# A two-layer mixer block and an attention block on one core: GpSimd's power products issued in four parts, and one reduction moved up

## The reference

```python
for layer in range(2):
    xn = rms_norm(h, attn_norm_g[layer])
    u_ssm, u_g, v_g, q, k, v = split(xn @ w_in[layer])
    y_ssm  = s5_mixer(u_ssm, ...)          # complex diagonal state space, 16 groups x 64 states
    y_sgu  = spatial_gating(u_g, v_g, ...)
    y_diff = diff_attention(q, k, v, ...)  # below
    h = h + concat(y_ssm, y_sgu, y_diff) @ w_out[layer]
    h = h + conv_gated_mlp(rms_norm(h, ffn_norm_g[layer]), ...)

def s5_mixer(...):
    a_bar = exp(lam * dt)
    b_bar = ((a_bar - 1) / lam) * b_mat
    states = associative_scan(a_bar, b_bar u)    # x_t = a x_(t-1) + b u_t, complex
    y = real(states @ c_mat) + d_skip * u
    y = gelu(y); return y * sigmoid(y @ w_glu + b_glu)

def diff_attention(...):
    q, k = rope(rms_norm(q)), rope(rms_norm(k))
    w = softmax(q1 k1) - lam * softmax(q2 k2)    # masked by chunks of 64
    out = w @ v
    return rms_norm(out, sub_gain) * (1 - lambda_init)
```

## Time and profile before

| | |
|---|---|
| profiled execution | 983.3 us, span 981.5 us |
| PE busy | 954.1 us, 97% of the span |
| weight loads (PEld) | 838.0 us, 85% |
| VectorE | 690.5 us, 70% |
| ScalarE | 547.4 us, 56% |
| GpSimd | 263.2 us, 27% |
| weight pairs | 294 loads of 512 KB, 3.5 us each to landing |
| chain that ended last | PE 86%, VectorE 8%, ScalarE 2%, GpSimd 1%, issue 1% |

### The profile page before, as it was taken

How to read it: one execution, slowest core, us unless ns; L and a number is a source line. 1 busy time by engine, 2 the same in 40 slices (tenths; PEclk the granted TensorE clock), 3 DMA queues, 4 the chain that set the end, 5 groups by cost and what they waited for, 6 DMA issues and landing times.

```text
span 981.5 us, 15775 instructions
## 1 busy us (share of the span) xinstructions
PE 954.1 (97%) x6139; PEld 838.0 (85%) x6143; DVE 690.5 (70%) x1074; ACT 547.4 (56%) x900; POOL 263.2 (27%) x196
## 2 busy tenths in 40 slices
PE   5979999999999999999999999999999999999997
PEld 4867789999978887899999988899777889888886
DVE  6998658776764689676777764558575845666785
ACT  7736556665744656766655654553444454555723
POOL 4891101677800021200555400003131300000030
PEclk9999999999999999999999999999999999999999
DMA  7722355655655552556655566565545445754462
GB/s 287 230 85 87 108 174 191 186 183 174 190 190 154 173 168 86 177 168 194 184 192 183 185 192 194 184 204 175 167 149 150 142 153 169 196 167 152 147 186 84
DMA packets 48473, 165.95 MB, mean 169 GB/s; under 512 B 6544, under 2 KB 7056, under 8 KB 48400
## 3 DMA queue, kind: packets, MB, share of 16 engines
q1 hardware_dynamic: 48400, 164.95, 53.0%
HBM read 162.83 MB, written 1.05 MB: 167 GB/s over the span
## 4 chain that ended last, share of the span: by engine, by line
PE 86%; DVE 8%; ACT 2%; POOL 1%; issue 1%; DMA 0%; DVEq 0%; POOLq 0%; SPq 0%; ACTq 0%
PE PJ L605 14%; PE PJ L607 13%; PE PJ L606 13%; PE PJ L596 10%; PE PJ L598 10%; PE PJ L597 10%; DVE wlo L1710 2%; PE PJ L557 2%; PE PJ L559 2%; PE PJ L558 2%; PE T L1045 1%; PE T L1036 1%; PE S L652 1%; DVE ropeq L1821 1%; PE T L974 1%
## 5 line engine op out<-in xcount | busy, mean ns | idle before, releaser
L1710 DVE TENSOR_TENSOR wlo<-raw,whi 128x1024 fp32r<-128x1024 f32 x294 | 366.9, 1280 | 87.1 <-ACT whi L1104 84.8
L1104 ACT ACTIVATE whi<-raw 128x1024 fp32r<-128x1024 f32 x294 | 302.5, 1062 | 73.6 <-DMA raw<-weights_in 64.7
L596 PE MATMUL PJ<-xthb,whi 128*128 128x256 f32 x864 | 243.1, 281 | 0.9 <-DVE wlo L1710 0.5
L598 PE MATMUL PJ<-xthb,wlo 128*128 128x256 f32 x864 | 242.3, 280 | 0.0
L597 PE MATMUL PJ<-xtlb,whi 128*128 128x256 f32 x864 | 241.5, 280 | 0.0
L605 PE MATMUL PJ<-whi,xthb 128*128 128x512 f32 (+1 forms) x432 | 174.3, 403 | 3.6 <-DVE wlo L1710 3.6
L607 PE MATMUL PJ<-whi,xtlb 128*128 128x512 f32 (+1 forms) x432 | 167.9, 389 | 0.0
L606 PE MATMUL PJ<-wlo,xthb 128*128 128x512 f32 (+1 forms) x432 | 167.7, 388 | 0.0
L596 PEld LDWEIGHTS PJ<-xthb,whi 128*128 128x128 f32 x864 | 163.0, 189 | 1.7 <-issue 1.5
L597 PEld LDWEIGHTS PJ<-xtlb,whi 128*128 128x128 f32 x864 | 163.0, 189 | 0.2
L598 PEld LDWEIGHTS PJ<-xthb,wlo 128*128 128x128 f32 x864 | 162.9, 189 | 0.0
(11 more groups left out here) (402 smaller groups left out, 1342.1 us busy)
## 6 DMA issues: line engine op xcount, KB each, us to landing
raw<-weights_in SPq DMA_DIRECT2D x294, 512.0 KB, 3.5
rt<-bmerge_in SPq DMA_DIRECT2D x6, 256.0 KB, 4.4
xres<-x_in SPq DMA_DIRECT2D x2, 512.0 KB, 5.5
memx<-mem_in SPq DMA_DIRECT2D x2, 512.0 KB, 4.1
y_out<-xn SPq DMA_DIRECT2D x4, 256.0 KB, 2.3
rowv<-rows_in SPq DMA_DIRECT2D x1, 576.0 KB, 10.5
ptmp<-bexp_in SPq DMA_DIRECT2D x2, 256.0 KB, 6.3
cex<-cexp_in SPq DMA_DIRECT2D x2, 256.0 KB, 8.5
```

The lines of the kernel that those rows point to most:

```text
L596: pe.matmul(o, a, xh[:, k, :], start=(first and f % 2 == 0), stop=False, skip_group_check=True)
L598: m = pe.matmul(o, b, xh[:, k, :], start=False, stop=last, skip_group_check=True)
L1104: act.activation(whi[:, p % HIGHS, :], raw[:, p % LOADS, :], ACT.Copy).then_inc(hi_ready, 1)
L1710: dve.tensor_tensor(wlo[:, p % LOADS, :], raw[:, p % LOADS, :], whi[:, p % HIGHS, :].bitcast(F32), ALU.subtract).then_inc(lo_ready, 1)
```

## The change

It has two edits.

`output_powers` and `input_powers` get an argument `parts`. With `parts=4` each of their products and sums over all 8 groups of states is issued as four instructions over 2 groups each, one step after the other (all four parts of a step, then the next step). The wait for the step before stands behind the last part only. The four calls of the first layer on GpSimd use 4; the calls for the second layer keep 1. The copy at the start of `input_powers` stays whole. The same elements are computed.

In VectorE's stream `diff_sums(1)` goes ahead of `diff_norm(0)`, in both layers, and the `lo_upto(s0 + 23)` between them is dropped, so that its split (slot 22) is made by `lo_upto(s0 + 24)` behind `diff_norm(1)`. In the second layer that split has already been made further up, and only the reduction moves.

```diff
-        def output_powers(eng, link, l, c, tmp, steps=(0, 1, 2)):
-
-            ar, ai = (wide(apw[:, c, 1:STEP + 1, 8 * l:8 * l + 8].rearrange("p t s -> p s t"), 32, 3) for c in range(2))
-            cr, nci = (wide(gpw[:, c, :, 0, :], STEP, 2) for c in range(2))
+        def output_powers(eng, link, l, c, tmp, steps=(0, 1, 2), parts=1):
+
             t = tmp.rearrange("p (s t h) -> p s t h", s=ST, t=STEP)
-            i0, k0, i1, k1, op = ((cr, ar, nci, ai, ALU.add), (nci, ar, cr, ai, ALU.subtract))[c]
-            o = gpw[:, c, :, 1:STEP + 1, :]
-            if 0 in steps:
-                link(eng.tensor_tensor(o, i0, k0, ALU.mult), False)
-            if 1 in steps:
-                link(eng.tensor_tensor(t, i1, k1, ALU.mult))
-            if 2 in steps:
-                link(eng.tensor_tensor(o, o, t, op))
...
+            w = ST // parts
+            for step in steps:
+                for at in range(0, ST, w):
+                    ar, ai = (wide(apw[:, k, 1:STEP + 1, 8 * l + at:8 * l + at + w].rearrange("p t s -> p s t"), 32, 3) for k in range(2))
+                    cr, nci = (wide(gpw[:, k, at:at + w, 0, :], STEP, 2) for k in range(2))
+                    i0, k0, i1, k1, op = ((cr, ar, nci, ai, ALU.add), (nci, ar, cr, ai, ALU.subtract))[c]
+                    o, tt_ = gpw[:, c, at:at + w, 1:STEP + 1, :], t[:, at:at + w, :, :]
+                    if step == 0:
+                        link(eng.tensor_tensor(o, i0, k0, ALU.mult), False)
+                    if step == 1:
+                        link(eng.tensor_tensor(tt_, i1, k1, ALU.mult), at + w == ST)
+                    if step == 2:
+                        link(eng.tensor_tensor(o, o, tt_, op), at + w == ST)
...
-            input_powers(pool, link, 0, 0, x_tile(0), ptmp)
-            input_powers(pool, link, 0, 1, x_tile(1), ptmp)
+            input_powers(pool, link, 0, 0, x_tile(0), ptmp, parts=4)
+            input_powers(pool, link, 0, 1, x_tile(1), ptmp, parts=4)
...
-            output_powers(pool, link, 0, 0, ptmp)
-            output_powers(pool, link, 0, 1, ptmp)
+            output_powers(pool, link, 0, 0, ptmp, parts=4)
+            output_powers(pool, link, 0, 1, ptmp, parts=4)
...
+                diff_sums(1)
                 diff_norm(0)
-                lo_upto(s0 + 23)
-                diff_sums(1)
                 diff_norm(1)
                 lo_upto(s0 + 24)
```

More of the change, by code:

```diff
@@ L402, in input_powers @@
-        def input_powers(eng, link, l, c, x, tmp, steps=(0, 1)):
-            ar, ai = (wide(apw[:, k, 1:STEP, 8 * l:8 * l + 8].rearrange("p t s -> p s t"), 32, 3) for k in range(2))
-            br, bi = (wide(bex[:, k, :, :], STEP - 1, 2) for k in range(2))
+            w = ST // parts
[11 more added lines that the diff above has]
+                        link(eng.tensor_tensor(o, o, tt_, op), at + w == ST)
@@ L406, in input_powers @@
+        def input_powers(eng, link, l, c, x, tmp, steps=(0, 1), parts=1):
             xv = x.rearrange("p (s t h) -> p s t h", s=ST, t=STEP)
             t = tmp[:, 0:ST * 96].rearrange("p (s t h) -> p s t h", s=ST, t=STEP - 1)
-            o = xv[:, :, 1:STEP, :]
-            i1, k1, op = (bi, ai, ALU.subtract) if c == 0 else (br, ai, ALU.add)
+            w = ST // parts
             if 0 in steps:
                 link(eng.tensor_copy(xv[:, :, 0, :], bex[:, c, :, :]), False)
-                link(eng.tensor_tensor(o, br if c == 0 else bi, ar, ALU.mult), False)
+            for step in ([0] if 0 in steps else []) + ([1, 2] if 1 in steps else []):
+                for at in range(0, ST, w):
+                    ar, ai = (wide(apw[:, k, 1:STEP, 8 * l + at:8 * l + at + w].rearrange("p t s -> p s t"), 32, 3) for k in range(2))
+                    br, bi = (wide(bex[:, k, at:at + w, :], STEP - 1, 2) for k in range(2))
+                    i1, k1, op = (bi, ai, ALU.subtract) if c == 0 else (br, ai, ALU.add)
+                    o, tt_ = xv[:, at:at + w, 1:STEP, :], t[:, at:at + w, :, :]
+                    if step == 0:
+                        link(eng.tensor_tensor(o, br if c == 0 else bi, ar, ALU.mult), False)
+                    if step == 1:
+                        link(eng.tensor_tensor(tt_, i1, k1, ALU.mult), at + w == ST)
+                    if step == 2:
+                        link(eng.tensor_tensor(o, o, tt_, op), at + w == ST)
```

## The result

| | changed | before | ratio, 95% interval |
|---|---|---|---|
| median of 20 runs each | 985.18 us | 983.63 us | 1.002, 1.001 to 1.0029 |
| lowest and highest | 981.56, 988.81 | 982.4, 986.6 | |
| profiled execution, span | 984.57, 982.7 | 983.3, 981.5 | |

The changed kernel is 1.5 us slower at the median where 5 us were forecast the other way; its runs also spread more widely than those of before. The profiled execution is 1.3 us above that of before, so it shows the size of the loss.

A forecast was written before the change was run, and what follows sets the result against it. TensorE, busy nearly throughout, bounds the kernel, so only its stops can be cut: 3.0 + 1.65 + 0.3 = 4.95 us off the profiled 983.3 gives 978.35, plus 0.74 for the median, 979.1 us; range 976.0 to 983.3.

The forecast's parts named there:

- Plus the extra VectorE turns ... from nothing to 2 us; I take 1.2: Output powers on GpSimd: splits and rope products falling into its work add 1.2 us, so the powers end at 75.3.
- The clock behind L680: PE's products with the output powers: no low-clock loss in the sum; a falling clock stood only as a rival, chance 0.2.
- I take 0.12 each, 4.4 us: GpSimd's powers in four parts: fixed cost of 36 more instructions, 4.4 us, between bounds of nothing and 5.9.
- A wait of up to half a microsecond: PE before the L671 transposes of the second input powers: may wait up to half a microsecond, against 2.8 us of cover.
- It would cost PE nothing further on if L680 waits anyway: The possible wait at the input powers' transposes, up to half a microsecond, costs PE nothing if L680 waits anyway.
- The stop at the keys goes, the 3.15 us stop before the first v pair goes, one of 3 us moves to the second: PE before L680: the 1.8 us L761 stop goes, the 3.15 shrinks to 0.6 or less, some 3 moves one pair on.
- the clock falls again: Rival, chance 0.2: the new 3 us stop lowers PE's clock, costing 2.3 us; L680 at 77.6, time 981.4 us.
- The powers eat the gain: Rival, chance 0.12: output powers come at 78.3, the powers' parts are worth nothing, time 982.1 us.
- Slower: GpSimd is locked out: Rival, chance 0.08: waiting GpSimd parts are passed over, 5.1 us each; two put the powers at 88.9, time 992.7 us.
- Edit 2: Attention's end: the 2.0 us stop before L829 goes, L1901 gives back 0.4, leaving 1.65; second layer gains 0.3.
- edit 1 was to bring PE 3.0 us earlier: Powers in four parts: L680 starts at 75.3 instead of 78.27, 3.0 us sooner, and all up to L829 moves with it.
- four signs of being wrong: Stop before L671 over 1 us; powers after 77; low-clock products before L680; parts over 0.75 us without VectorE beside them.

The follow-up runs named there:

- edit 1 alone: The changed kernel with the old order of the sums at the attention's end, all powers in four parts: 988.16 us, ratio 1.0042.
- edit 2 alone: The changed kernel with parts=1 in all four calls, keeping the sums of the second tile first: 980.7 against 983.51 us, ratio 0.997.
- the early lambda products: Sums-first kernels with lambda products moved up behind the coefficients: two parts 981.0 us, whole powers 990.12, two parts for output powers only 984.32, two parts plus earlier split 980.98.
- the kernel whose scans wait: The changed kernel with VectorE's two scans held back until GpSimd's output powers are done: 982.96 against 983.03 us, ratio 0.9997.
- the lambda products late: The changed kernel with the lambda products moved behind VectorE's two splits: 985.46 us, ratio 1.0021.

## Why the prediction was wrong, by its own steps

- **"Plus the extra VectorE turns ... from nothing to 2 us; I take 1.2": this step failed.** By the prediction's own sum the output powers end at 72.77 - 3.05 + 5.3 (the measured fixed part, below, in full) = 75.0, plus the turns; they end at 80.28, which leaves at least 5.3 us for the turns. The table puts 4.0 of them inside the output powers. I had counted two splits and some rope products at the front and had sent VectorE ahead by up to 4 us in the next paragraph, but did not ask what it would then do: its splits of v, the scans and the split behind them come into the last GpSimd sums (6.47 us). Of the range from nothing to 2, neither end was right; letting the scans alone wait took 2.8 us off.
- **The clock behind L680 was put at nothing in the sum** (it stood as a rival). It took 1.7 us in the changed kernel.
- **"I take 0.12 each, 4.4 us": near enough.** Four parts of 192 take 1.96 us (19.97) where the whole took 1.53, so 0.143 per added instruction. For 256 it is 2.41 against 1.97 for the same product whole, in the second layer of before (below), so 0.147. 36 of them make 5.3 us if none is hidden, 0.9 more; but beside VectorE's instructions a part fills only 0.3 to 0.45 of 0.60 us, so there most of it is hidden, as the lower bound of the prediction had it. How many parts that is true of was not counted.

```profile
236.15 1.97 POOL L396 TENSOR_TENSOR gpw<-gpw,apw 128x1024 f32<-128x1024 f32 x1
```

- **"A wait of up to half a microsecond" before the input powers' transposes**: 2.17 us. The second set was ready at 38.0 instead of 33.3: 18 x 0.143 = 2.6 of fixed part and 2 of turns, against 2.8 of cover. "It would cost PE nothing further on if L680 waits anyway" held in form (L689 did wait), for the wrong reason.
- **The stop at the keys goes, the 3.15 us stop before the first v pair goes, one of 3 us moves to the second**: right, 0, 0 and 2.93 us, and VectorE's instructions shrank as listed. PE was done with that pair at about 78.0 (77.58 + 0.40), 2.7 us after the forecast 75.3: 1.8 of it is the low clock, the rest the stop at the input powers.
- **The rival "the clock falls again"** came on top, twice: the second v pair took 4.6 us for 2.8, the products with the powers 5.6 for 3.9. Its argument against itself, that the 2.0 us stop before L829 was followed by no such pace, was luck of that trace: with edit 1 alone the same stop of 2.02 us was followed by a low clock. The spell that the rival meant, in the second v pair, decided nothing, since PE had to wait for the powers behind it; the one that cost time is that behind L689, after PE's stop for the late powers. **"The powers eat the gain"** named the mechanism with 78.3 for the powers and no loss; they came 2.0 us after that.
- **"Slower: GpSimd is locked out"** was not it. No part waits 5 us; in the worst row, 6.47 us, four parts (2.41) give way to four instructions of VectorE in turn. The loss came from many ordinary turns, not from a lockout.
- **Edit 2**: forecast 1.65 and 0.3. At L838 2.1 us are won and 0.4 given back at 118.45, hence 1.7, as laid out; in the second layer the weight load of L838 still waits, 0.36 instead of 0.52 us, so 0.2. The medians say 2.8 to 3.0 with intervals of about 1 us. Beside the parts (3.0) the low clock behind the old stop explains 1.3; alone (2.8) the spans of the traces differ by 2.3, and the rest is not explained. VectorE sums early and makes both splits behind the norms, as laid out:

```profile
112.21 0.69 DVE L1896 TENSOR_REDUCE hss<-qh 128x4 f32<-128x512 f32 x1
...
114.40 1.13 DVE L1903 SCALAR_TENSOR_TENSOR xn<-T,hr,rowv 128x128 f32<-128x128 f32 x4 [0.47 <-POOL hr L1633]
115.44 2.35 DVE L1719 TENSOR_TENSOR wlo<-raw,whi 128x1024 fp32r<-128x1024 f32 x2
```

Put together at the profiled executions: edit 1 was to bring PE 3.0 us earlier behind the powers and brought it 3.9 later, 6.9 apart; of these, 5.2 are L689's start (80.47 against 75.3, the powers' lateness) and 1.7 the low clock behind it. 3.9 less 1.7 for edit 2, less 0.8 found later and less 0.2 in the second layer, is the 1.2 us of the spans. Of the prediction's four signs of being wrong three came: a stop of over 1 us before the input powers' transposes, powers after 77, low-clock products before L680. Not settled is why the changed kernel's runs spread over 7 us where those of edit 2 alone spread over 0.6 (980.5 to 981.05, 7 runs). A clock that falls behind a stop in one execution and not in another, for 1.3 to 2.1 us each time, is one candidate, and that the alternation of two late engines falls out differently each time is another; neither is shown.

## What to carry to other kernels

Where two engines exclude each other, shortening one's instructions can hand its time to the other, as it did here: before cutting an instruction into parts, ask when the one that is cut must be done, and list what the other engine will do with its head start until then. Cut only so far that the cut engine is through before that work arrives; here two parts were free, four cost 4.5 us and eight 11 to 12. A move of a few us on the shared pair can cost more than the moved work, as the early lambda products did, so the place of each two-input VectorE instruction against GpSimd's stream is part of its price. An engine that is held back to make room is late for its own next hand-over, as the scans that waited were. A reduction that another engine waits for, moved ahead of work with slack, gave 2.8 us here.

## What the runs showed of the hardware

- An added GpSimd instruction costs 0.14 to 0.15 us, at 192 and at 256 elements, with nothing beside it. Where VectorE and GpSimd alternate most of it is hidden: pairs of instructions follow each other every 1.58 us, 1.14 to 1.24 of it VectorE's, and the part's own length alone is 0.60.
- Two scans of 128 x 512, which take 2.48 us when GpSimd is done (79.72 in the kernel whose scans wait), take 3.36 beside its parts. So scans lose time beside GpSimd as products do.
- While GpSimd makes a root (3.11 us for 128 x 16), VectorE's two-input instructions are not held up: in the changed kernel a split beside it takes 1.22 us, its bare time:

```profile
53.37 3.11 POOL L1543 TENSOR_TENSOR hr<-hr,mhalf 128x16 f32<-128x16 f32 x1
```

```profile
54.33 1.22 DVE L1719 TENSOR_TENSOR wlo<-raw,whi 128x1024 fp32r<-128x1024 f32 x1
```

- A stop of 3.2 us in the kernel whose scans wait was followed by no low clock (1.00 in 60 to 80), one of 2.93 in the changed kernel was. Two stops of 2.02 us at the attention's end differ in the same way (1.00 behind the one of before, 0.58 with edit 1 alone), and of 2.17 and 2.15 us at the input powers (1.00 in 36 to 42 in the changed kernel, 0.82 with the lambda products late). The length of the stop alone did not decide it here.
